# Seven half-size products in place of eight for the branch-gate projections of a hybrid attention, delta-net and mixture-of-experts block

## The reference, cut to what matters

```
h      = rms_norm(x)
proj   = h @ w_in                       # 1024 x 5640, all columns of the block
         # dq dk dv | gq gk gv beta decay gate | m_gate_a (1024) | m_gate_b (1024)
y_a    = diff_attention(dq, dk, dv)      # 4 heads, softmax minus lambda softmax
y_b    = gated_delta_net(...)            # chunks of 64 tokens, triangular solve, state
merged = sigmoid(m_gate_a) * (y_a @ w_branch_attn) + sigmoid(m_gate_b) * (y_b @ w_branch_gdn)
x      = x + merged @ w_out
x      = x + hier_moe(rms_norm(x))       # 32 experts of 1024 -> 256 (gate, up) -> 1024 (down)
out    = rms_norm(x)
```

## Time and profile before

| what | value |
|---|---|
| median of 3 runs | 463.12 us (462.32 to 463.28) |
| the profiled execution: its time, its span | 462.34 us, 460.5 us |
| PE busy | 427.2 us (93%), 4311 matmul instructions |
| DVE, ACT, POOL busy | 205.3 us (45%), 120.3 us (26%), 10.1 us (2%) |
| mean granted PE clock | 0.983 of full speed |
| read from HBM | 134.59 MB |
| branch-gate projections and what stands between them | 117.4 to 194.8 us |
| branch products | 194.8 to 223.3 us |
| experts | from 264.8 us |

### The profile page before, as it was taken

How to read it: one execution, slowest core, us unless ns; L and a number is a source line. 1 busy time by engine, 2 the same in 40 slices (tenths; PEclk the granted TensorE clock), 3 DMA queues, 4 the chain that set the end, 5 groups by cost and what they waited for, 6 DMA issues and landing times.

```text
span 460.5 us, 10231 instructions
## 1 busy us (share of the span) xinstructions
PE 427.2 (93%) x4311; PEld 335.0 (73%) x4311; DVE 205.3 (45%) x561; ACT 120.3 (26%) x311; POOL 10.1 (2%) x26
## 2 busy tenths in 40 slices
PE   8999999999999999999999889899999996779673
PEld 7885698874778788888888677586776865547351
DVE  3367377995234442613222545354534442333133
ACT  5002523100214133220012523233323331222144
POOL 4010100000000000000000000000000000000001
PEclk9999999999999999999999899999999998899899
DMA  8969967716605052255599899999999999999992
GB/s 309 410 223 329 412 221 235 280 56 180 233 0 184 1 182 78 106 184 182 173 422 406 317 381 423 418 420 421 421 422 422 424 422 421 422 421 422 419 388 101
DMA packets 38178, 136.88 MB, mean 297 GB/s; under 512 B 8576, under 2 KB 9920, under 8 KB 26240
## 3 DMA queue, kind: packets, MB, share of 16 engines
q1 hardware_dynamic: 33792, 135.22, 74.4%
q10 hardware_dynamic: 4352, 1.21, 1.2%
HBM read 134.59 MB, written 1.84 MB: 296 GB/s over the span
## 4 chain that ended last, share of the span: by engine, by line
PE 71%; DMA 16%; DVE 8%; issue 2%; ACT 1%; ACTq 0%; POOLq 0%; DVEq 0%; SPq 0%
PE ps L892 24%; PE ps L1299 11%; DMA arena<-in_moe_w_up 7%; PE ps L1163 6%; PE ps L1147 6%; DMA ring<-in_moe_w_up 6%; PE ps L1342 4%; PE ps L1258 4%; PE ps L1352 4%; DVE arena L1689 2%; DVE arena L1686 2%; DMA arena<-in_w_in 2%; PE ps L1307 1%; PE ps L910 1%; DVE arena L1578 1%
## 5 line engine op out<-in xcount | busy, mean ns | idle before, releaser
L892 PE MATMUL ps<-arena 128*128 128x256 f32 (+1 forms) x640 | 156.3, 402 | 0.8 <-DMA arena<-in_w_in 0.8
L892 PEld LDWEIGHTS ps<-arena 128*128 128x128 f32 x640 | 119.9, 190 | 29.8 <-issue 14.1
L1299 PE MATMUL ps<-arena 128*32 128x128 f32 x1040 | 37.3, 282 | 10.2 <-DMA arena<-in_moe_w_up 7.2
L1299 PEld LDWEIGHTS ps<-arena 128*32 128x32 f32 x1040 | 29.3, 110 | 16.5 <-DMA arena<-in_moe_w_up 7.7
L689 ACT ACTIVATE gains<-ps 32x256 f32<-32x256 f32 x62 | 23.4, 377 | 54.3 <-PE ps L1342 53.9
L1299 PE MATMUL ps<-ring,arena 128*32 128x128 f32 x768 | 28.2, 286 | 4.4 <-DMA ring<-in_moe_w_up 3.2
L2015 DVE TENSOR_TENSOR masks<-ps,masks 128x64 f32<-128x64 f32 x32 | 7.2, 225 | 53.4 <-ACT masks L670 53.2
L2031 DVE COPY arena<-ps 32x256 f32<-32x256 f32 x62 | 25.8, 416 | 11.4 <-PE ps L1342 10.5
L1163 PE MATMUL ps<-arena 128*128 128x256 f32 x128 | 29.3, 383 | 0.0
L1299 PEld LDWEIGHTS ps<-ring,arena 128*32 128x32 f32 x768 | 22.3, 112 | 8.5 <-issue 5.4
L1258 PE MATMUL ps<-masks,arena 128*128 128x128 f32 x224 | 27.8, 283 | 0.4 <-issue 0.4
(11 more groups left out here) (302 smaller groups left out, 468.3 us busy)
## 6 DMA issues: line engine op xcount, KB each, us to landing
arena<-in_moe_w_down SPq DMA_DIRECT2D x19, 1024.0 KB, 25.0
...
```

The lines of the kernel that those rows point to most:

```text
L892: last = pe.matmul(out, lhs, rhs, start=(k == 0 and (i > 0 or part % 2 == 0)), stop=(k == KD - 1), skip_group_check=(i == 0))
L1299: last = pe.matmul(c.ps[ROWS * q:ROWS * (q + 1), i % 2, 0:P], c.Hg[:, k, ROWS * i:ROWS * (i + 1)], w[:, :, start:start + 127:2], start=(k ...
```

## The change

Each gate chunk (512 output columns by 1024 features, times 1024 features by 256 tokens) is cut into quarters: outputs in halves of 256 columns, features in halves of four slabs, tokens in halves of 128. Seven products of quarter by quarter (the Winograd form of Strassen's scheme) take the place of eight. Each product is 8 matmuls that stream 128 tokens, that is 16 instructions. `P6` and `P7` add onto the bank of `P1`, `P3` onto that of `P5`.

- POOL forms `T1`, `T3`, `T2`, `T4` (128x512) once from `hT`, and for each chunk `S1`, `S2`, `S4`, `S3` (128x1024) from the weights. They lie in `ring[2]`, expert 2's slot.
- ACT copies four results for each chunk to SBUF (128x256 each), and the sigmoid is taken there later (128x1024).
- DVE adds three times for each chunk: `C11` and `C12` (128x256), `C2` (128x512).
- PE waits for the forms, for copies before it adds onto a bank, and for copies and adds of the chunk before to free banks.
- Expert 2 is loaded after expert 3, behind the branch products, and expert 4 waits for `merged_ready` 2. The gate results lie in other buffers; two semaphore pairs are merged (`idle_ready` into `eps_ready`, `lambda_loaded` into `router_loaded`, so L1610 waits for all nine of these loads).

The diff, cut to its core (`product_done`, `copied`, `added` and `combined` give the count of a signal that the named step reaches):

```diff
-PARTS = [4 if c[3] == "T" else 2 for c in CHUNKS]
+SEVEN = ("ma0", "ma1", "mb0", "mb1")
+ORDER = ("P1", "P2", "P5", "P6", "P4", "P3", "P7")
+COPIED = ("P1", "P5", "P6", "P4")
+ADDED = ("C11", "C12", "C2")
+COMBINED = ("S1", "S2", "S4", "S3")
+FORMS = {"P1": ("A11", "B11"), "P2": ("A12", "B21"), "P5": ("S1", "T1"), "P6": ("S2", "T2"), "P4": ("A22", "T4"),
+         "P3": ("S4", "B22"), "P7": ("S3", "T3")}
+BANK_OF = {"P1": 0, "P6": 0, "P7": 0, "P2": 1, "P5": 2, "P3": 2, "P4": 3}
+BANKS = {"ma0": (2, 0, 3, 1), "ma1": (0, 3, 2, 1), "mb0": (3, 2, 0, 1), "mb1": (1, 2, 0, 3)}
+PARTS = [7 if c[0] in SEVEN else 4 if c[3] == "T" else 2 for c in CHUNKS]
...
-    c.mg = [at(n, 1024) for n in ("mg0", "ck", "vb", "gate")]
+    c.mg = [at(n, 1024) for n in ("mg0", "cv", "ck", "vb")]
+    c.merged = [at(n, 1024) for n in ("mg0", "ck")]
+    c.form = {n: v3(ring[:, OWN - 1, 1024 * i:1024 * i + 1024], 4) for i, n in enumerate(COMBINED)}
+    for i, n in enumerate(("T1", "T2", "T4", "T3")):
+        c.form[n] = v3(ring[:, OWN - 1, 4096 + 512 * i:4608 + 512 * i], 4)
+    for i in range(2):
+        for j in range(2):
+            c.form[f"B{i + 1}{j + 1}"] = c.hT[:, 4 * i:4 * i + 4, P * j:P * j + P]
...
-    for j in range(1, OWN):
-        load_expert(j)
-        load_chunk(2 + j)
-    load_chunk(5)
+    load_expert(1)
+    for i in (3, 4, 5):
+        load_chunk(i)
...
     sp.wait_ge(s["yaT_ready"], 1)
     load_expert(3)
+    load_expert(OWN - 1)
+    sp.wait_ge(s["merged_ready"], 2)
     load_expert(4)
...
+    form = c.form
+    pool.wait_ge(s["hT_ready"], 1)
+    pool.tensor_tensor(form["T1"], form["B12"], form["B11"], ALU.subtract).then_inc(s["forms_combined"], 1)
+    pool.tensor_tensor(form["T3"], form["B22"], form["B12"], ALU.subtract).then_inc(s["forms_combined"], 1)
+    pool.wait_ge(s["forms_combined"], 1)
+    pool.tensor_tensor(form["T2"], form["B22"], form["T1"], ALU.subtract).then_inc(s["forms_combined"], 1)
+    pool.wait_ge(s["forms_combined"], 3)
+    pool.tensor_tensor(form["T4"], form["B21"], form["T2"], ALU.subtract).then_inc(s["forms_combined"], 1)
+    for n_, name in enumerate(SEVEN):
+        i = CI[name]
+        w = weight_quarters(c, i)
+        def free(product):
+            if n_:
+                pool.wait_ge(s["proj_ready"], product_done(SEVEN[n_ - 1], product))
+        pool.wait_ge(s[f"stage_loaded{i % 2}"], 16 * (i // 2 + 1))
+        free("P5")
+        pool.tensor_tensor(form["S1"], w["A21"], w["A22"], ALU.add).then_inc(s["forms_combined"], 1)
+        pool.wait_ge(s["forms_combined"], combined(name, "S1"))
+        free("P6")
+        pool.tensor_tensor(form["S2"], form["S1"], w["A11"], ALU.subtract).then_inc(s["forms_combined"], 1)
+        pool.wait_ge(s["forms_combined"], combined(name, "S2"))
+        free("P3")
+        pool.tensor_tensor(form["S4"], w["A12"], form["S2"], ALU.subtract).then_inc(s["forms_combined"], 1)
+        free("P7")
+        pool.tensor_tensor(form["S3"], w["A11"], w["A21"], ALU.subtract).then_inc(s["forms_combined"], 1)
...
+def weight_quarters(c, i):
+    w = c.stage[i % 2][:, 0:KD * 512].rearrange("p (k n) -> p k n", k=KD)
+    return {f"A{a + 1}{j + 1}": w[:, 4 * j:4 * j + 4, TOK * a:TOK * a + TOK] for a in range(2) for j in range(2)}
+def quarters(c, name):
+    out = c.mg[SEVEN.index(name)].rearrange("p (a f) -> p a f", a=4)
+    return {f"C{a + 1}{j + 1}": out[:, 2 * a:2 * a + 2, P * j:P * j + P] for a in range(2) for j in range(2)}
+def product_out(c, name, product):
+    return c.quarter_bank[BANKS[name][BANK_OF[product]]]
...
+    def copy_product(name, product, quarter):
+        act.wait_ge(s["proj_ready"], product_done(name, product))
+        act.activation(quarters(c, name)[quarter], product_out(c, name, product), ACT.Copy).then_inc(s["product_copied"], 1)
+    def sigmoid_of(name):
+        n_ = SEVEN.index(name)
+        act.wait_ge(s["quarter_added"], added(name, "C2"))
+        act.activation(c.mg[n_], c.mg[n_], ACT.Sigmoid).then_inc(s["mg_ready"], 1)
...
+            if m == 0 and between:
+                between()
+    copy_product("ma0", "P1", "C11")
+    copy_product("ma0", "P5", "C22")
+    copy_product("ma0", "P6", "C12")
+    copy_product("ma0", "P4", "C21")
     act.wait_ge(s["TT_ready"], 2)
     exps(0)
-    evacuate("ma0", c.mg[0], "mg_ready", ACT.Sigmoid)
+    copy_product("ma1", "P1", "C11")
+    copy_product("ma1", "P5", "C22")
+    copy_product("ma1", "P6", "C12")
+    copy_product("ma1", "P4", "C21")
     act.wait_ge(s["aT_in"], 1)
-    act.wait_ge(s["side_ready"], SI["aT0"] + 1)
-    exps(1)
     act.wait_ge(s["side_ready"], SI["z1"] + 1)
-    evacuate("ma1", c.mg[1], "mg_ready", ACT.Sigmoid)
-    evacuate("mb0", c.mg[2], "mg_ready", ACT.Sigmoid)
+    copy_product("mb0", "P1", "C11")
+    exps(1, lambda: copy_product("mb0", "P5", "C22"))
+    copy_product("mb0", "P6", "C12")
+    sigmoid_of("ma0")
+    copy_product("mb0", "P4", "C21")
+    sigmoid_of("ma1")
...
     act.activation(c.flat["Yb"], c.flat["F"], ACT.Square).then_inc(s["oa_squares"], 1)
+    copy_product("mb1", "P1", "C11")
+    sigmoid_of("mb0")
+    copy_product("mb1", "P5", "C22")
     act.wait_ge(s["oa_root"], 1)
     act.activation(c.ra, c.ra, ACT.Sqrt).then_inc(s["oa_root"], 1)
     act.wait_ge(s["gate_ready"], 2)
     act.activation(c.flat["A"], c.flat["TT"], ACT.Square).then_inc(s["ob_squares"], 1)
     act.wait_ge(s["ob_root"], 1)
     act.activation(c.rb, c.rb, ACT.Sqrt).then_inc(s["ob_root"], 1)
+    copy_product("mb1", "P6", "C12")
     act.wait_ge(s["side_ready"], SI["yaT"] + 1)
     act.activation(c.flat["qT"], c.side[side_pair("yaT")], ACT.Copy).then_inc(s["yaT_ready"], 1)
-    act.wait_ge(s["yb_ready"], 1)
-    evacuate("mb1", c.mg[3], "mg_ready", ACT.Sigmoid)
+    copy_product("mb1", "P4", "C21")
+    sigmoid_of("mb1")
...
+    def bank_free(name, product):
+        if name == "ma0":
+            if product == "P1":
+                pe.wait_ge(s["pair_free1"], CI["ma0"] // 2)
+            elif product == "P2":
+                pe.wait_ge(s["pair_free0"], CI["dv"] // 2 + 1)
+            return
+        prev = SEVEN[SEVEN.index(name) - 1]
+        bank, was = BANKS[name][BANK_OF[product]], BANKS[prev]
+        if bank == was[3]:
+            pe.wait_ge(s["product_copied"], copied(prev, "P4"))
+        else:
+            pe.wait_ge(s["quarter_added"], added(prev, ("C2", "C11", "C12")[was.index(bank)]))
+    def products(name, *wanted):
+        i = CI[name]
+        forms = dict(c.form, **weight_quarters(c, i))
+        for product in wanted:
+            held, streamed = FORMS[product]
+            if product == "P1":
+                pe.wait_ge(s[f"stage_loaded{i % 2}"], 16 * (i // 2 + 1))
+            if product in ("P1", "P2", "P5", "P4"):
+                bank_free(name, product)
+            if product == "P6":
+                pe.wait_ge(s["product_copied"], copied(name, "P1"))
+            elif product == "P3":
+                pe.wait_ge(s["product_copied"], copied(name, "P5"))
+            elif product == "P7":
+                pe.wait_ge(s["product_copied"], copied(name, "P6"))
+            if held in COMBINED:
+                pe.wait_ge(s["forms_combined"], combined(name, held))
+            out = product_out(c, name, product)
+            begins = product in ("P1", "P2", "P5", "P4")
+            for a in range(2):
+                for k in range(4):
+                    last = pe.matmul(out[:, a, :], forms[held][:, k, a * P:(a + 1) * P], forms[streamed][:, k, :],
+                                     start=(begins and a == 0 and k == 0), stop=(k == 3), skip_group_check=True)
+            last.then_inc(s["proj_ready"], 1)
...
+    products("ma0", "P3")
     scores(0)
-    project("ma0", 3)
+    products("ma0", "P7")
+    products("ma1", "P1")
     solve(0)
-    project("ma1", 0)
+    products("ma1", "P2", "P5")
     turn_probs(0)
     first_outputs_and_state()
-    project("ma1", 1)
+    products("ma1", "P6", "P4")
     weigh_values(0)
     keys_on_state()
-    project("ma1", 2)
+    products("ma1", "P3", "P7")
     solve(1)
+    products("mb0", "P1")
     scores(1)
-    project("ma1", 3)
+    products("mb0", "P2", "P5")
     second_outputs()
-    project("mb0", 0)
-    project("mb0", 1)
+    products("mb0", "P6", "P4")
     turn_probs(1)
-    project("mb0", 2)
+    products("mb0", "P3", "P7")
     weigh_values(1)
-    project("mb0", 3)
-    project("mb1", 0)
-    project("mb1", 1)
+    products("mb1", "P1", "P2", "P5", "P6", "P4")
     pe.wait_ge(s["ya_ready"], 1)
     turn("yaT", lambda i: c.oa[:, i % 2, (i // 2) * P:(i // 2 + 1) * P])
-    project("mb1", 2)
-    project("mb1", 3)
+    products("mb1", "P3", "P7")
...
-        if j == 0:
-            pe.wait_ge(s[f"pair_free{1 - half}"], (NCH + half) // 2)
+        if n == 0:
+            pe.wait_ge(s["product_copied"], copied("mb1", "P4"))
+            pe.wait_ge(s["quarter_added"], added("mb1", "C11"))
+        elif n == 1:
+            pe.wait_ge(s["quarter_added"], added("mb1", "C2"))
...
```

(59 more changed lines are left out.)

16 lines of the change are left out of this document (5 added, 11 removed).

## The result

The kernel with the seven products takes 467.61 us (median of 4 runs, 467.08 to 469.45), the kernel before 462.72 in the runs beside it (4 runs, 461.54 to 463.28): ratio 1.0088, 95% interval 1.0052 to 1.0124. It is slower by 0.9%, 4.9 us between the medians and 4.1 by the ratio. The forecast was +2.8 us.

What follows compares the result with a forecast made beforehand. Engines bound the first half, expert-weight transfers the second, joined by SP's queue. Gains 5.4 + 2.0 less new waits 3.5 and hold 2.5 leave -1.4; +4.2 for expert 2 gives +2.8: 465.9 us, range 462.6 to 467.8.

Steps and rivals of the forecast that it cites:

- the gate stretch: From the first product of `ma0` to the first branch product on PE; forecast 1.4 us shorter.
- the debt: Expert 2's 3 x 1.049 MB issued behind the branch products lengthen SP's queue: +4.2 us, bounds 3.4 to 5.3.
- the hold: POOL's forms make DVE's scalings within SBUF wait, at two places that matter: 2.5 us, bounds 0 to 2 x 1.89.
- the clock falls: Rival, chance 0.10: PE's clock falls around its 2.7 us wait before `turn_probs(1)`, costing 1.7 us; 467.6 us.
- Products: On PE, 28 products at 1.78 us replace 16 parts at 3.455: gain 5.4 us, 2.5 at the worse pace.
- No saving: Rival, chance 0.03: 28 products on PE cost what 16 parts did; 468.8 us at the pace of L1258.
- Old waits: PE's waits of 0.93, 0.93 and 0.24 us among the gate parts mostly go: gain 2.0 us.
- New waits: PE waits 0.8 before `turn_probs(1)`, 0.9 before `yaT`, 1.8 before `P7` of `mb1`: 3.5 us together.
- DVE beside POOL: The term for the hold: 0.6 us at `maxima(0)`, 1.9 more before `turn_probs(1)`; 2.5 us taken.
- two holes: Gaps in SP's queue at 252 to 256 and 267 to 269 us, to absorb 2.3 and 0.9 us.
- Costs set to nothing: ACT's 16 copies, DVE's 12 adds, merged semaphores and the `merged_ready` wait were said to cost nothing.

Runs made afterwards that it cites:

- the run without holds: Changed kernel with three waits added on POOL, so that no form runs beside DVE's small scalings; 464.17 us, ratio 1.0013.
- all three edits: Changed kernel with expert 2 loaded early, POOL waits added, and ACT's root table load and `P6` copy moved earlier; 458.22 us, ratio 0.9887.
- the last one: The kernel with all three edits, plus `P3` of `mb0` moved ahead of `turn_probs(1)` on PE; 456.1 us, ratio 0.9845.

## Why the prediction was right or wrong

The direction was right, and for the reason given, the late load. The other term came out with the wrong sign: the gate stretch was to be 1.4 us shorter and is 0.7 longer. 467.6 lies in the range, near its upper end, and above the 467.5 that the prediction gave as the end of the forecast's own bounds. Those bounds were too narrow: they come to the debt's two ends and 0.5 us more on either side, though three waits might each be 0.5 off and the hold had a bound of 3.8 us. With these at their worst the same sum gives 463.12 + 1.4 + 5.3 = 469.8. The rise was put too small, 2.8 us against 4.1 to 4.9. The rival *the clock falls* named 467.6, the measured value, and that is in part luck: it had the debt 1.2 us too large, the gate stretch and its start 0.7 too small, and nothing for the 0.9 behind the last load's issue and outside the span; and it set the median 0.8 above the profiled execution, where it stands 0.3. Point by point:

- **Products.** 3.74 us for two, 183.14 to 186.71 by their starts: 1.785 each against 1.78. *No saving* falls.
- **Old waits.** Both of 0.93 are gone, as said. In the place of the third, and of the 0.6 for the late scaling in `maxima(0)`, stand 0.15 and 0.16.
- **New waits.** `turn_probs(1)` 2.98 against 2.7; `yaT` 0.88 against 0.9; the last `P7` 1.31 against 1.8. All the waits together are 5.5 against 6.1 us, so they were slightly over-estimated.
- **DVE beside POOL.** Shown from both sides: taking POOL away gives the old durations back, putting it into the old kernel makes the hold. The price of a form was mis-sized, 1.89 from a square of one tile with itself; with two different inputs it is 2.35. That moved the hold from 1.9 to 2.17.
- **The clock.** This is the step that failed. The forecast gave it nothing and left it to a rival of 0.10; it fell, and cost 1.5 us in the profiled execution. It fell behind waits of 2.98, 2.97 and 3.31 in three profiles, and not behind 2.97 in a fourth nor behind 0.81. A wait of nearly 3 us deserved a share of that cost in the sum. How often it falls behind this wait stays open, as the mean clocks of the other executions do not say where they were low.
- **Restarts.** The stretch was to be 77.25 - 1.4 = 75.85 us and is 77.91, 2.06 more. The clock adds 1.5 and the waits take off 0.6, so 1.2 are left. The same sum leaves 0.9 in the run without holds, 0.5 with all three edits and 0.4 in the last one; their waits are three (0.81, 0.88, 1.32), three (0.15, 0.81, 0.33) and one (0.33). A product behind a wait takes 1.89 (193.74 to 195.63) instead of 1.785. I infer that a wait costs 0.1 to 0.2 more than its length; I did not test it by itself, and the rest does not go by the number of waits. Some 0.3 of it is in every changed kernel: 28 products at 1.785 instead of 1.78 are 0.1, and `P3` of `ma0`, now between two small 64-row steps, takes 1.98 (131.39 to 133.37), 0.2 more.
- **Expert 2's debt.** The sum said 4.2, bounds 3.4 to 5.3. From expert 3's issue to the last load's, the five kernels with the late load take 199.0 to 200.2 us and the five with the early one (the kernel before among them) 195.3 to 197.0. The means, 199.3 and 196.2, are 3.1 apart; by the medians of the two runs that change nothing else it is 3.3 and 4.0. The sum took two holes into account, 3.2 us. The slow spells on either side filled too, as the windows from 224 to 300 us show, of before and of after:

```profile
224.00:260.00 36.00, 34.56 (x195) 31.03 (x195) 11.98 (x49) 8.70 (x16) 0.00 (x0) 1.00 0.96 377
260.00:300.00 40.00, 36.50 (x646) 26.90 (x648) 16.91 (x61) 12.11 (x41) 0.00 (x0) 0.96 0.99 400
```

```profile
224.00:260.00 36.00, 34.56 (x192) 30.94 (x191) 11.80 (x46) 7.75 (x14) 0.00 (x0) 1.00 0.97 395
260.00:300.00 40.00, 38.42 (x723) 28.94 (x721) 20.03 (x72) 14.21 (x47) 0.00 (x0) 1.00 1.01 416
```

  That is 18 x 36 + 16 x 40 = 1,288 thousand bytes more, or 3.1 us at 422 GB/s, and the queue began 0.96 us later; so by this count about 4 us of the 7.45 were absorbed and 3.4 stayed. The sum had 4.2; the debt was over-sized by 0.8 to 1.2.
- **Costs set to nothing.** ACT's copies, DVE's adds and the other forms cost nothing outside the named places. One more step was held, the subtraction L1888 with two inputs in SBUF: 1.84 us (0.69 before), and no wait of PE stands behind it until 139.35.
- **What is left.** 0.70 of the 4.94 us stands behind the last load's issue. In the ten profiles this tail is 39.7 to 41.9 us long, with no order by kernel (40.5 before, 41.2 after), so I give it no cause.

Where did the saving of the seven products go? In the gate stretch 5.4 + 2.1 us were gained (products and old waits), and 5.5 in five waits, 1.5 in the clock and 1.2 in restarts took them back; behind it, the late load took 3 to 4 us more. With those mended the change is worth 6.9 us. I count 5.4 of it to the seven products, by their length on PE. The 2.1 of the old waits come from putting other work ahead of `scores`; whether a new order of the eight parts alone would have won them too was not tested.
